# The final RMSNorm of a decoder step: row-major blocks through fp32 transposes, replaced by channel-major tiles with ones-matmul sums

## What is computed

```python
def rmsnorm(x, g):
    xf = x.astype(jnp.float32)
    y = xf * lax.rsqrt(jnp.mean(xf * xf, axis=-1, keepdims=True) + EPS)
    return (y * g.astype(jnp.float32)).astype(x.dtype)

def sq_relu_mlp(u, w_up, w_down):
    h = jax.nn.relu(jnp.einsum('btd,df->btf', u, w_up))
    return jnp.einsum('btf,fd->btd', h * h, w_down)

def trunk(x, ...):
    for i in range(DEPTH):                  # DEPTH = 2
        u = rmsnorm(x, g_mix[i])
        ...                                 # pooling mixer (layer 0) or short convolution (layer 1)
        x = x + mem_attend(rmsnorm(x, g_attn[i]), mem_k[i], mem_v[i], w_q[i], w_o[i])
        x = x + sq_relu_mlp(rmsnorm(x, g_ffn[i]), w_up[i], w_down[i])     # D_FF = 4096
    return rmsnorm(x, g_final), ...
```

## Time and profile before

| | |
|---|---|
| median of the runs, lowest | 1608.88 us, 1604.48 us |
| profiled execution: span of the slowest core (core 2) | 1604.9 us |
| spans of the 8 cores in that execution | 1589.7 to 1604.9 us |
| PE busy | 1546.0 us, 96% of the span |
| DVE, ACT, POOL busy | 848.0, 567.6, 114.1 us |
| fp32 transposes of the final blocks | 136 (17 blocks of 8) |
| last quarter of the second MLP from the first final block's place | 1502.6 us to the end |

### The profile page before, as it was taken

One profiled execution on the slowest core, in us unless ns is written; L12 is line 12 of the kernel. 1 busy time (PEld: TensorE's weight loads), 2 busy tenths in 40 slices (PEclk: granted clock), 3 DMA queues, 4 the chain that ended last, 5 costly groups with the idle time before them and its releaser, 6 DMA issues.

```text
span 1604.9 us, 28273 instructions; the slowest of 8 cores (1589.7 to 1604.9 us)
## 1 busy us (share of the span) xinstructions
PE 1546.0 (96%) x10154; PEld 899.5 (56%) x10154; DVE 848.0 (53%) x1924; ACT 567.6 (35%) x1071; POOL 114.1 (7%) x245
## 2 busy tenths in 40 slices
...
GB/s 223 213 113 157 190 200 129 124 162 105 78 61 131 114 1 106 13 94 110 1 1 1 1 1 147 160 216 129 161 135 90 74 103 53 14 1 1 40 67 107
DMA packets 91860, 153.58 MB, mean 96 GB/s; under 512 B 4894, under 2 KB 42014, under 8 KB 91708
## 3 DMA queue, kind: packets, MB, share of 16 engines
...
...
## 4 chain that ended last, share of the span: by engine, by line
PE 85%; DMA 5%; DVE 4%; ACT 2%; issue 2%; POOL 0%; DVEq 0%; ACTq 0%; SPq 0%; POOLq 0%
PE PS L293 82%; DMA MEM<-cv 3%; DVE MEM L328 3%; PE PS L297 2%; ACT MEM L320 2%; DMA MEM<-gv 1%; PE PS L302 1%; DMA MEM<-x 1%; DVE MEM L332 1%; ACT MEM L309 1%; DVE MEM L340 0%; DVE MEM L346 0%; POOL MEM L355 0%; ACT MEM L344 0%; DVEq L1419 0%
## 5 line engine op out<-in xcount | busy, mean ns | idle before, releaser
L293 PE MATMUL PS<-MEM 128*128 128x416 bf16 (+6 forms) x8874 | 1462.0, 325 | 7.8 <-DVE MEM L346 3.0
L293 PEld LDWEIGHTS PS<-MEM 128*128 128x128 bf16 (+1 forms) x8874 | 827.7, 98 | 628.8 <-issue 34.9
L332 DVE TENSOR_TENSOR MEM<-PS,MEM 128x416 f32<-128x416 f32 (+6 forms) x558 | 312.6, 576 | 346.8 <-PE PS L293 278.5
L320 ACT ACTIVATE MEM<-PS 128x416 f32<-128x416 f32 (+5 forms) x469 | 238.8, 510 | 571.2 <-PE PS L293 559.9
L332 DVE TENSOR_TENSOR MEM<-MEM 128x416 bf16<-128x416 f32 (+3 forms) x282 | 161.3, 585 | 238.6 <-ACT MEM L320 228.5
L320 ACT ACTIVATE MEM<-MEM 128x416 bf16<-128x416 f32 (+9 forms) x299 | 185.5, 630 | 142.1 <-DVE MEM L332 111.7
L328 DVE SCALAR_TENSOR_TENSOR MEM<-MEM 128x416 bf16<-128x416 f32 (+7 forms) x322 | 177.0, 601 | 60.3 <-ACT MEM L320 50.4
L297 PE MATMUL PS<-MEM 128*128 128x128 bf16 (+6 forms) x1096 | 73.8, 265 | 26.2 <-DVE MEM L340 9.6
L305 DVE SCALAR_TENSOR_TENSOR MEM<-MEM 128x256 f32<-128x256 f32 x256 | 90.8, 420 | 4.1 <-DMA MEM<-qrows 4.1
L344 ACT COPY MEM<-PS 128x512 f32<-128x512 f32 (+3 forms) x73 | 39.2, 536 | 124.3 <-PE PS L293 113.4
L297 PEld LDWEIGHTS PS<-MEM 128*128 128x128 bf16 (+3 forms) x1096 | 51.9, 104 | 48.4 <-issue 47.4
...
## 6 DMA issues: line engine op xcount, KB each, us to landing
MEM<-ck SPq DMA_DIRECT2D x64, 512.0 KB, 8.2
MEM<-cv POOLq DMA_DIRECT2D x64, 256.0 KB, 8.5
...
MEM<-x SPq DMA_DIRECT2D x16, 512.0 KB, 13.7
...
MEM<-w_up POOLq DMA_DIRECT2D x32, 256.0 KB, 20.4
MEM<-qrows SPq DMA_DIRECT2D x32, 256.0 KB, 8.1
```

What stands on the lines that cost most here:

```text
L293: P.add(PE, "c", lambda e, o=out.ap, l=lhsT.ap, r=rhs.ap: e.matmul(out=o, lhsT=l, rhs=r, start=start, stop=stop), [lhsT, rhs], [out])
L320: P.add(ACT, "c", lambda e, o=out.ap, i=in_.ap: e.activation(out=o, in_=i, func=func, bias=bias, scale=sc), rd, [out])
L332: P.add(eng, "c", lambda e, o=out.ap, a=in0.ap, b=in1.ap: e.tensor_tensor(out=o, in0=a, in1=b, op=op), [in0, in1], [out])
```

## The change

The output is left channel-major: `y` becomes [1024, 2048] in device memory, and the host turns it. The final norm works on the tiles as they lie:

- squares of a tile by two ACT instructions of 4 chunks each (`sq`), then `norm_p` and `norm_r` of the other norms, then for each chunk one DVE multiplication of X, gain and reciprocal root (`scale`), and for each two chunks one store. Chunks named in `onpool` take two instructions instead: a POOL multiplication and an ACT scaling by the gain.
- Tiles 0, 1 and 2 are threaded into the next stA and stB by `fill`, tile 3 into stB of tile 4 (with `pace` an item may go behind every group there). Tile 4 is normalised in two parts: `rest` (272 columns) and `last` (128 columns, with 8 ones-matmuls of full width instead of `norm_p` and `norm_r`).
- Two buffers of one tile each (`OUT`) are used in turn: tiles 0 and 2 and the rest take the first, tiles 1 and 3 and the last part the second.

```diff
-    y_d = dout("y", [SEQ, D])
-    ys_d = dout("ys", [NS, D])
+    y_d = dout("y", [D, SEQ])
+    ys_d = dout("ys", [D, NS])
...
-            if (c in (1, 4, 6) or l == 1 and c == 3 and len(fill) > 2) and not todo and fill:
+            if (c in (1, 4, 6) or pace or l == 1 and c == 3 and len(fill) > 2) and not todo and fill:
...
     def finish_phase():
...
-            for c in range(NCH):
-                tp(PSv(b0 + c // 4, (c % 4) * 128, (c % 4 + 1) * 128, m=m), X(c, sl(a, b)), IDF())
...
-            sumsq(SQT(p=(0, m)), rows, ss(0))
-            act(ss(1), ss(0), AF.Ln, scale=1.0 / D, bias=EPS)
-            act(ss(2), ss(1), AF.Exp, scale=-0.5)
-            stt(st(p=(0, m)), rows, ss(2), GB(p=(0, m)), ALU.mult, ALU.mult)
-            dma(SP, DV(ys_d if a >= SEQ else y_d[a:b, :]), st(p=(0, m)), f"stg{k}")
...
+        def store(a, b, out, c0, c1):
+            m = min(b, SEQ)
+            for o_d, u0, u1, o0 in ((y_d, a, m, 0), (ys_d, max(a, SEQ) - SEQ, b - SEQ, max(a, SEQ))):
+                if u1 > u0:
+                    w = out(sl(c0, c1), sl(max(o0 - a, 0), max(o0 - a, 0) + u1 - u0))
+                    dma(SP, DV(o_d.rearrange("(c p) t -> p c t", p=128)[:, c0:c1, u0:u1]), w, f"out{ctr[0] % 2}")
+
+        def block(a, b, SQ, onpool=()):
+            n = b - a
+            k = ctr[0] % 2
+            ctr[0] += 1
+            RS = RST[k]
+            out = OUT[k] if n == TW else T(OUT[k].off, F32, [NCH, n])
+
+            def sq(c0, c1):
+                act(SQ(sl(c0, c1)), X(sl(c0, c1), sl(a, b)), AF.Square)
+
+            def scale(cs):
+                for c in cs:
+                    g = G(c, sl(R_FINAL, R_FINAL + 1))
+                    if c in onpool:
+                        tt(out(c), X(c, sl(a, b)), RS(sl(0, n)), ALU.mult, eng=POOL)
+                        act(out(c), out(c), AF.Copy, scale=g)
+                    else:
+                        stt(out(c), X(c, sl(a, b)), g, RS(sl(0, n)), ALU.mult, ALU.mult)
+                for c in cs[::2]:
+                    store(a, b, out, c, c + 2)
+
+            return sq, lambda: norm_p(0, SQ, RS, n), lambda: norm_r(0, SQ, RS, n), scale, RS
+
+        def tile(ti):
+            a, n = TILES[ti][0], TILES[ti][1]
+            sq, p, r, scale, _ = block(a, a + n, U3[ti], onpool=(2, 3, 6, 7) if ti == NT - 2 else ())
+            its = [lambda: sq(0, 4), lambda: sq(4, 8)]
+            if ti == NT - 2:
+                return its + [None, None, p, None, r, None, lambda: scale((0, 1, 2, 3)), lambda: scale((4, 5, 6, 7))]
+            return its + [p, r] + [lambda c=c: scale((c, c + 1)) for c in range(0, NCH, 2)]
+
+        def rest():
...
+            sq, p, r, scale, _ = block(t0 + TAIL, t0 + n, SQ, onpool=(3, 6, 7))
+            return [lambda: sq(0, 4), lambda: sq(4, 8), None, p], [r, lambda: scale(range(NCH))]
+
+        def last():
...
+            sq, _, _, scale, RS = block(t0, t0 + TAIL, SQ, onpool=(3, 5, 7))
+
+            def stat():
+                bk = nxt()
+                for c in range(NCH):
+                    mm(PSv(bk, 0, TAIL), ONESB(), SQ(c), c == 0, c == NCH - 1)
+                act(PSv(bk, 0, TAIL), PSv(bk, 0, TAIL), AF.Ln, scale=1.0 / D, bias=EPS)
+                act(RS(sl(0, TAIL)), PSv(bk, 0, TAIL), AF.Exp, scale=-0.5)
+
+            return sq, stat, scale
...
     for at in attn_phase(1, fill):
         if at == (2, NT - 1):
-            final_block = finish_phase()
-        elif at == (3, NT - 1):
-            fill.append(lambda: final_block(done[0], done[0] + TAIL))
...
+            f_tile, f_rest, f_last = finish_phase()
+        elif at and at[0] == "A" and at[1] == 4 * NT - 1:
+            pace.append(1)
         elif at and at[0] == "T":
...
+            now, after = f_rest()
+            fill.extend(now)
+        elif at and at[0] == 3 and at[1] < NT - 1:
+            fill.extend(f_tile(at[1]))
     for f in fill:
-        f()
+        if f is not None:
+            f()
+    f_sq, f_stat, f_scale = f_last()
+    f_sq(0, 6)
+    f_sq(6, 8)
+    after[0]()
+    f_stat()
+    after[1]()
+    f_scale(range(NCH))
```

More of the change, by code:

```diff
@@ L460, in build_program @@
     late = []
+    pace = []
     def project(Wt, memn, dst, st, od, k, chan):
@@ L1332, in finish_phase @@
     def finish_phase():
[L1333 to L1339, removed]
-        ctr = [0]
[L1342 to L1347, removed]
-            for c in range(NCH):
-                tp(PSv(b0 + c // 4, (c % 4) * 128, (c % 4 + 1) * 128, m=m), X(c, sl(a, b)), IDF())
+        OUT, RST = [], []
@@ new lines, in finish_phase @@
+        for i in range(2):
+            o = claim(f"final{i}").off
+            OUT.append(T(o, F32, [NCH, TW]))
+            RST.append(T(o + OUT[i].nbytes, F32, [TW]))
+        ctr = [0]
+        def store(a, b, out, c0, c1):
[4 more added lines that the diff above has]
+                    dma(SP, DV(o_d.rearrange("(c p) t -> p c t", p=128)[:, c0:c1, u0:u1]), w, f"out{ctr[0] % 2}")
@@ L1350, in final_block @@
+        def block(a, b, SQ, onpool=()):
+            n = b - a
             k = ctr[0] % 2
             ctr[0] += 1
-            st = STG[k]
-            rows = V(PS[0:m, b0:b0 + 2, :].rearrange("p a b -> p (a b)"), PSv(b0, 0, 1).ivs + PSv(b1, 0, 1).ivs, True)
-            ss = lambda i: SSs(k, sl(i, i + 1), p=(0, m))
-            sumsq(SQT(p=(0, m)), rows, ss(0))
-            act(ss(1), ss(0), AF.Ln, scale=1.0 / D, bias=EPS)
-            act(ss(2), ss(1), AF.Exp, scale=-0.5)
-            stt(st(p=(0, m)), rows, ss(2), GB(p=(0, m)), ALU.mult, ALU.mult)
@@ L1359, in final_block @@
-            dma(SP, DV(ys_d if a >= SEQ else y_d[a:b, :]), st(p=(0, m)), f"stg{k}")
-        return final_block
+            RS = RST[k]
[12 more added lines that the diff above has]
+                    store(a, b, out, c, c + 2)
@@ new lines, in rest @@
+        def rest():
+            t0, n = TILES[NT - 1][0], TILES[NT - 1][1]
+            SQ = T(U3[NT - 1].off, BF16, [NCH, n - TAIL])
+            sq, p, r, scale, _ = block(t0 + TAIL, t0 + n, SQ, onpool=(3, 6, 7))
+            return [lambda: sq(0, 4), lambda: sq(4, 8), None, p], [r, lambda: scale(range(NCH))]
+        def last():
+            t0 = TILES[NT - 1][0]
+            SQ = T(U3[NT - 1].off + NCH * (TILES[NT - 1][1] - TAIL) * 2, BF16, [NCH, TAIL])
+            sq, _, _, scale, RS = block(t0, t0 + TAIL, SQ, onpool=(3, 5, 7))
[6 more added lines that the diff above has]
+            return sq, stat, scale
@@ L1363, in build_program @@
+        return tile, rest, last
     prelude()
```

23 lines of the change are left out of this document (5 added, 18 removed).

## The result

The changed kernel took 1617.72 us (median), before took 1607.53 us in the same job: a ratio of **1.0066**, 95% interval 1.0046 to 1.0087. (One of the four runs of before, 1828.39 us, was in a slow state that some runs of this program show, whatever the kernel; it stands in the median, but not in the ratio.) It is slower by some 10.6 us, less than 2%, but outside the forecast range of 1596 to 1614 us.

What follows compares the result with a forecast made beforehand. PE, busy 96% of the span, was taken as the bound up to the end, where an ACT, DVE and store chain ends the program. +1.0 us up to T1 and +1.0 behind it on 1604.9 gave 1607 us, range 1596 to 1614.

Steps and rivals of the forecast that it cites:

- The removed and the added work: PE up to T1: nine transpose blocks go (7.8 us), three norm_p and their extra matmuls come (2.5 us), −5.4 us.
- T1: The end of stB of tile 3, at 1574.75 us in the earlier profile; the program then ended 30.15 us later.
- The squares: stA of tiles 0 to 2: PE waits at norm_p for ACT's second square, 2.0 to 2.2 us per tile.
- Three tiles: 6.3 us: PE's waits for the squares at the three norm_p ahead of T1, added up as 6.3 us.
- So T1 moves by −7.8 + 2.5 + 6.3: Sum up to the end of stB of tile 3: transposes removed, norm work added, waits for squares; +1.0 us.
- From T1 to the end: Tile 3's norm, rest, last part and stores: 31.2 us instead of 30.15, +1.0 us, the 2.6 us wait included.
- the store: stB of tile 3: DVE's pairs of scalings wait for the preceding store's landing, 2.6 us each; PE then stands 2.6 us.
- the store's landing decides: Slower rival: three landings in a row on DVE take 3.7 us instead of 2.6, 3.3 us more, 1610.4 us; chance 0.22.
- the port: SBUF rule: a DVE instruction with two SBUF inputs excludes a POOL instruction that reads SBUF; the first issued keeps the ports.
- the series as a rival: Slower rival: POOL also waits for DVE's four scalings in tile 3's batch, +4.2 us in all, 1609 us; chance 0.1.
- the last scalings: End of program: DVE's 3.55 us and POOL's 2.8 us in series, last issue at T1 + 27.9, end at T1 + 31.2.
- Both rivals on the slow side: Store landings of 3.7 us (1610.4 us, chance 0.22) and POOL waiting for DVE in tile 3's batch (1609 us, chance 0.1).

Runs made afterwards that it cites:

- the refined version: The change with squares early, own store channels and no POOL, plus norm_r later, tile 3's second scalings later, four-chunk stores: 1595.33 us, ratio 0.9918.

## Why the prediction was wrong

**The removed and the added work: nearly right.** −7.8 + 2.5 = −5.4 us was forecast for PE up to T1. Where PE stands nowhere, in the refined version, it is 70.12 − 74.95 = −4.8.

**The squares: right in place and size, wrong in what they cost.** 2.0, 2.0 and 2.2 us of stand were forecast (6.2 us, put down as 6.3), 1.94, 1.94 and 2.02 measured. The step that failed is "Three tiles: 6.3 us" and the sum that takes it up, "So T1 moves by −7.8 + 2.5 + 6.3": it counted a stand at its length. PE behind a stand of this length runs at half clock for about 3 us in two cases of three, 1.7 us each. With the two falls of core 4 (3.4 us) +1.0 becomes +4.4; measured +4.75. The sum took the clock as 1.00 throughout, though the earlier trace rows shows 0.88 for the part of the kernel before in which PE stands.

**From T1 to the end: every wait at its place, nearly all too short.** Times of core 4 behind T1, forecast and measured:

| point | forecast | measured | added here |
|---|---|---|---|
| squares of chunks 4 to 7 of tile 3 done | 7.45 | 8.99 | 1.54 |
| root of tile 3 | 11.25 | 14.63 | 1.84 |
| fourth POOL multiplication done | 15.1 | 20.01 | 1.53 |
| squares of the rest done | 17.9 | 22.75 | −0.06 |
| last scalings begin | 20.8 | 26.98 | 1.33 |
| end | 31.2 | 37.90 | 0.52 |

The first row is the store: a pair's scalings, SP's issue (0.37 us, which the sum left out) and the landing follow one another, and the chain of waits shows 3.06, 3.15 and 2.98 us where 2.6 was put (the sum's own steps, such as 4.75 to 7.45, come to 2.7). That was the rival "the store's landing decides", 1.1 us of the 3.3 that it was priced at. The second is nearly all the clock again: 7.59 us for the 74 matmuls behind the stand of 4.12 us, 5.99 without it. The third is the port. In tile 3's batch the prediction put DVE and POOL side by side and kept the series as a rival, at 4 x 0.55 = 2.2 us more (+4.2 in all). That rival is what happened, a little cheaper: they take turns, and POOL's four multiplications take 5.18 us where 3.84 was scaled, three waits of 0.45 us for a scaling. The Trainium skill (SBUF — State Buffer, "Who interferes with whom") says that the port pair which the two engines share is an exclusive lock, and that a DVE instruction with two SBUF inputs contends with a POOL instruction that reads SBUF; the turns agree with it. In the last scalings the prediction put them in series. From there to the end it came near (10.4 us forecast, 10.9 measured) partly by luck: DVE was done after 5.6 us and not 6.35, but SP's last issue ended 2.8 us behind that and not 0.75. In the fifth row PE's stands ahead of the rest's `norm_p` (4.98 + 0.47 us, forecast 4) leave its last matmuls at a lower clock (0.54 on the mean from 1597 to 1602 us), and they follow one another to the root; how the 1.33 us divide between the two is not shown.

**The sum.** On core 4, 4.75 − 1.0 = 3.75 us up to T1 and 6.7 us behind it are 10.4 us more than forecast. Core 4 is one of the longer cores; the mean of eight, 116.5 us, lies 9.4 us over the forecast's 107.1. That 1607 + 10.4 = 1617.4 comes so near the measured median of 1617.72 is luck: the profiled execution itself spans 1613.1 us, because core 4 came to stA of tile 2 at 1495.50 us, 4.3 us earlier than the core of before. Both rivals on the slow side were there in part, and the range had room for both in full (1607 + 3.3 + 2.2 = 1612.5). What carried the time out of the range is the clock, which no rival named: 3.4 us up to T1 and 1.6 us in the second row, on core 4.
